# First four output blocks of four projections computed side by side over the input tiles, and the opening's conditioning rows in two channel halves

## The reference, cut to what matters

```python
for l in range(2):
    cond = silu(c) @ w_ada[l] + b_ada[l]              # 1024 -> 3 x 1024
    shift, scale, gate_raw = split(cond, 3)
    h = x * (1 + scale) + shift
    proj = h @ w_in[l]                                # 1024 -> 6272 columns
    p_hg, p_rw, p_gate = split(proj)                  # p_rw: r, k, v, z, decay/icl rank
    ...                                               # HGRN2, RWKV7 scans, branches
    x = layer_norm(DN_ALPHA * x + (1 + gate_raw) * (merged @ w_out[l]))
h = rms_norm(x); u = h @ lru_w_in                     # 1024 -> 2 x 1536
xb = conv4(u[:1536]); ...                             # RG-LRU, back to x
h = rms_norm(x); u = h @ ret_w_in; q, k = rotary(...) # retention, 4 heads, back to x
```

## Time and profile before

| | us |
|---|---|
| median of 3 runs | 2222.09 (2217.86 to 2224.73) |
| the profiled execution's own time | 2224.56 |
| its span | 2222.8 |
| PE busy | 1934.4 |
| DVE / ACT / POOL busy | 962.9 / 869.0 / 607.8 |

### The profile page before, as it was taken

The page is one execution under the profiler, slowest core; times in us unless marked ns, Lnnn a source line. Parts: engine busy times, 40 slices in busy tenths (PEclk is TensorE's granted clock), DMA queues, the critical chain, the costliest instruction groups (busy, mean ns, idle before and its releaser), DMA issues.

```text
span 2222.8 us, 35507 instructions
## 1 busy us (share of the span) xinstructions
PE 1934.4 (87%) x14368; PEld 1534.2 (69%) x14368; DVE 962.9 (43%) x1299; ACT 869.0 (39%) x1244; POOL 607.8 (27%) x255
## 2 busy tenths in 40 slices
PE   1999988899787998988899797989597998998987
PEld 1876877798565866877798574865474886777755
DVE  5326375632456126375632434737604123232232
ACT  1333456433323334456433324256515323333322
POOL 0333422200252433422300231422141441322212
PEclk9999999999898999999999899999799999999999
DMA  8232222200364322222200323211132231212112
GB/s 333 84 101 64 93 86 71 67 4 13 127 261 156 104 68 67 90 85 71 67 4 13 133 95 133 95 57 48 61 101 95 95 99 43 86 47 66 56 58 77
DMA packets 57524, 192.80 MB, mean 87 GB/s; under 512 B 5408, under 2 KB 5664, under 8 KB 54976
## 3 DMA queue, kind: packets, MB, share of 16 engines
q1 hardware_dynamic: 57408, 191.10, 25.5%
HBM read 173.25 MB, written 17.83 MB: 86 GB/s over the span
## 4 chain that ended last, share of the span: by engine, by line
issue 51%; PE 29%; POOL 9%; DVE 5%; ACT 3%; DMA 1%; POOLq 0%; DVEq 0%; ACTq 0%; SPq 0%
PE proj L1690 17%; POOL w_lo_sb L625 9%; PE aux L1850 2%; PE aux L1781 2%; DVE area_sb L1106 2%; DMA slots_sb<-w_ada 1%; PE aux L1907 1%; PE proj L1850 1%; PE aux L1904 1%; DVE area_sb L1109 1%; DVE slots_sb L1109 1%; ACT L720 1%; DVE act_lo_sb L1106 0%; DVE slots_sb L1106 0%; ACT L810 0%
## 5 line engine op out<-in xcount | busy, mean ns | idle before, releaser
L625 POOL TENSOR_TENSOR w_lo_sb<-w_raw_sb,w_hi_sb 128x1024 fp32r<-128x1024 f32 x231 | 589.6, 2553 | 1404.1 <-ACT w_hi_sb L700 1404.1
L1690 PE MATMUL proj<-act_hi_sb,w_hi_sb 128*128 128x512 f32 x1784 | 730.3, 409 | 97.4 <-DVE act_lo_sb L1106 63.5
L1690 PE MATMUL proj<-act_lo_sb,w_hi_sb 128*128 128x512 f32 x1784 | 707.3, 396 | 0.0
L1690 PE MATMUL proj<-act_hi_sb,w_lo_sb 128*128 128x512 f32 x1784 | 707.2, 396 | 0.0
L700 ACT ACTIVATE w_hi_sb<-w_raw_sb 128x1024 fp32r<-128x1024 f32 x231 | 244.4, 1058 | 740.4 <-PE proj L1690 687.0
L1690 PEld LDWEIGHTS proj<-act_hi_sb,w_hi_sb 128*128 128x128 f32 x1784 | 343.1, 192 | 192.3 <-issue 63.0
L1690 PEld LDWEIGHTS proj<-act_lo_sb,w_hi_sb 128*128 128x128 f32 x1784 | 343.3, 192 | 74.0 <-issue 6.3
L1690 PEld LDWEIGHTS proj<-act_hi_sb,w_lo_sb 128*128 128x128 f32 x1784 | 342.5, 192 | 74.2
L1106 DVE TENSOR_TENSOR area_sb<-area_sb 128x256 f32<-128x256 f32 (+2 forms) x208 | 141.3, 718 | 20.0 <-ACT area_sb L835 11.8
L1106 DVE TENSOR_TENSOR slots_sb<-slots_sb 128x512 f32<-128x512 f32 (+1 forms) x64 | 73.7, 1155 | 64.1 <-ACT slots_sb L795 26.1
L1106 DVE TENSOR_TENSOR area_sb<-area_sb,slots_sb 128x512 f32<-128x512 f32 (+1 forms) x90 | 72.1, 816 | 49.7 <-ACT slots_sb L722 38.7
(11 more groups left out here) (234 smaller groups left out, 2328.1 us busy)
## 6 DMA issues: line engine op xcount, KB each, us to landing
w_raw_sb<-wall SPq DMA_DIRECT2D x231, 512.0 KB, 3.5
slots_sb<-w_ada SPq DMA_DIRECT2D x8, 1536.0 KB, 7.3
slots_sb<-w_ada SPq DMA_DIRECT2D x8, 1024.0 KB, 5.9
gate_scr<-stage_sb SPq DMA_DIRECT2D x32, 256.0 KB, 2.2
slots_sb<-gate_scr SPq DMA_DIRECT2D x32, 256.0 KB, 4.0
x_scr<-area_sb SPq DMA_DIRECT2D x3, 2048.0 KB, 7.5
area_sb<-x_scr SPq DMA_DIRECT2D x3, 2048.0 KB, 9.5
area_sb<-x_t SPq DMA_DIRECT2D x2, 2048.0 KB, 9.6
```

The costliest lines, as they stand in the source:

```text
L625: nc.gpsimd.tensor_tensor(w_lo[:, b % 2, :, :].rearrange("p k n -> p (k n)"), w_raw[:, b % 2, :], w_hi[:, b % 2, :, :].rearrange("p k n -> ...
L1690: ins = MM(bank, w[:, s, k, :], a[:, t, :], start=(start and i == 0), stop=(stop and i == len(terms) - 1))
```

## The change

In four places (rw in layers 0 and 1, `lru_in`, the first head's `ret_in`) the first four output blocks are computed together. Their weights are laid out anew: piece p of the group holds input tiles 2p and 2p + 1 of all four blocks. TensorE takes input tile after input tile and does its three terms for all four blocks, 12 matmuls, into four `aux` banks (`project_group`); it counts a piece as used behind every second tile. The block of `w_down` and `a_down`, first until now, becomes the fifth. ScalarE's calls of `weights` for the group's third to fifth piece stand between its `high` calls, and the one for the sixth ahead of the four copies out. The loops lose one turn.

In the opening the shift and scale rows are loaded and added up in two halves of 512 channels each, eight parts of 512 KB a half, six buffers, x tile by tile between them. VectorE makes the first four tiles of h ahead of the second half's steps; TensorE's column sums of the second half stand between the group's fourth and fifth tile. The gate's columns come in two transfers, and its eight steps sit behind the first two blocks of each of three turns and two at the end. Elsewhere bank numbers and counts follow.

```diff
+    def side_by_side(blocks):
+
+        grouped.append(len(pieces))
+        return [[blocks[m][2 * p + k] for k in range(2) for m in range(4)] for p in range(4)]
...
-        rw = [full("w_in", l, 4096)]
+        rw = side_by_side([full("w_in", l, 2048 + P * m) for m in range(4)])
+        rw += [full("w_in", l, 4096)]
...
-        jobs.add(("ada", l), 0)
+        for half in range(1 if l else 2):
+            jobs.add(("ada", l, half), 4 + half)
+        for i in range(4):
+            jobs.add(("rw", l, i), i, signalled=False)
...
-            return b if b < first["lru_out", 0][0] else b - 4
+            return b - 4 * sum(b > g for g in grouped) - 4 * (b >= first["lru_out", 0][0])
...
+        def group_ready(eng, name):
+
+            eng.wait_ge(block_used, first[name[:2]][0] + 4)
+            return aux[jobs(name)[0]][:, :]
...
-            sp.dma_start(xa[:, :, :], dram["x_t"].rearrange("k p t -> p k t")).then_inc(S("x_in"), 16)
-
-            def load_ada(l, k):
-                n = 8 * l + k
-                wait(sp, S("ada_used"), n - 1)
-                cols = slice(0, ADA if l else 2 * D)
-                sp.dma_start(ada_in[:, k % 2, cols], dram["w_ada"][l, k][:, cols]).then_inc(S(f"ada_in{k % 2}"), 16)
-
+
+            def load_part(half, k):
+                n = KT * half + k
+                wait(sp, S("ada_used"), n - 5)
+                sp.dma_start(ada_part[:, n % 6], dram["w_ada"][0, k][:, D * half:D * half + D])\
+                    .then_inc(S(f"ada_part{n % 6}"), 16)
+
+            def load_x(m):
+                sp.dma_start(xa[:, m, :], dram["x_t"][m]).then_inc(S(f"x_first{m}"), 16)
+
+            def load_ada(k):
+                wait(sp, S("ada_used"), 2 * KT + k - 1)
+                sp.dma_start(ada_in[:, k % 2], dram["w_ada"][1, k]).then_inc(S(f"ada_in{k % 2}"), 16)
+
+            for k in range(6):
+                load_part(0, k)
+            load_x(0)
+            load_x(1)
+            blocks_to(1)
+            load_part(0, 6)
+            load_part(0, 7)
+            load_x(2)
+            load_x(3)
+            blocks_to(2)
             for k in range(KT):
-                if k == 6:
-                    blocks_to(2)
-                load_ada(0, k)
+                load_part(1, k)
+            for m in range(4, KT):
+                load_x(m)
...
-                    sp.dma_start(hg.rearrange("p (k h) t -> p k (h t)", k=KT),
-                                 dram["w_ada"][0].rearrange("k p n -> p k n")[:, :, 2 * D:]).then_inc(S("gate_cols"), 16)
+                    for half in range(2):
+                        sp.dma_start(hg[:, 8 * half:8 * half + 8].rearrange("p (k h) t -> p k (h t)", k=4),
+                                     dram["w_ada"][0, 4 * half:4 * half + 4].rearrange("k p n -> p k n")[:, :, 2 * D:])\
+                            .then_inc(S("gate_cols"), 16)
+                        blocks_to(6 + half)
...
@@ ScalarE
+                    if m > 2 and m % 2:
+                        weights(b_rw + m // 2 + 1)
+                weights(b_rw + 5)
...
+                for i in range(4):
+                    x = group_ready(act, ("rw", l, i))
+                    if i > 1:
+                        evacuated_job(act, ("rw", l, i - 2))
+                    A(ST[(b_rw + i) % 2], x, ACT.Copy, scale=V(f"mu{l}", 1 + i)).then_inc(S("mu_scaled"), 1)
+                for i in (2, 3):
+                    evacuated_job(act, ("rw", l, i))
+                b = b_rw + 4
...
+            for i in range(4):
+                x = group_ready(act, ("lru_in", 0, i))
+                act.wait_ge(S("conv_done"), i + 1)
+                job_read(A(ST[(LRU + i) % 2], x, ACT.Copy), ("lru_in", 0, i))
...
@@ VectorE
+            conditioned(0, 0, ((0, 4), (8, 4)))
+            for m in range(5):
+                if m < 4:
+                    modulated(0, m)
+                if m:
+                    low(SPLITS["h", 0] + m - 1, m - 1, ST[(m - 1) % 2])
+            for k in range(KT):
+                ada_part_step(1, k)
...
-                with dve.Fori(0, 4) as turn:
+                    dve.wait_ge(S("gate_cols"), 32)
+                with dve.Fori(0, 3) as turn:
                     for j in range(4):
-                        shifted(b + j, 1 + j, slots[:, turn, j, :], turn)
-                        if l == 0 and j % 2:
-                            k = 2 * turn + j // 2
+                        shifted(b + j, 5 + j, slots[:, turn + 1, j, :], turn)
+                        if l == 0 and j < 2:
+                            k = 2 * turn + j
                             dve.wait_ge(S("gate_rows"), k + 1)
                             stt(xa[:, 4:6, :], hg[:, bass.ds(2 * k, 2), :], derived[:, bass.ds(derived_column("c") + k, 1)], xa[:, 4:6, :],
                                 ALU.mult, ALU.add).then_inc(S("gate_rows"), 1)
+                if l == 0:
+                    for k in (6, 7):
+                        dve.wait_ge(S("gate_rows"), k + 1)
+                        stt(xa[:, 4:6, :], hg[:, 2 * k:2 * k + 2, :], DV["c"][:, k:k + 1], xa[:, 4:6, :],
+                            ALU.mult, ALU.add).then_inc(S("gate_rows"), 1)
...
+            for j in range(4):
+                evacuated_job(dve, ("lru_in", 0, j))
+                convolved(X_C[:, j, :], (LRU + j) % 2, [V("conv_w", RT * k + j) for k in range(4)], V("conv_b", j))
+            with dve.Fori(0, RT // 4 - 1) as turn:
...
@@ TensorE
+            def project_group(phase, layer, ready):
+
+                b = first[phase, layer][0]
+                banks = [job_open(pe, (phase, layer, i)) for i in range(4)]
+                for k in range(KT):
+                    s = (b + k // 2) % 2
+                    ready(k)
+                    if k % 2 == 0:
+                        pe.wait_ge(lo_ready, b + k // 2 + 1)
+                    pe.wait_ge(split_lo, SPLITS[("h", layer) if phase == "rw" else phase[0:3] + "_h"] + k + 1)
+                    for i in range(4):
+                        at = 4 * (k % 2) + i
+                        for n, (w, a) in enumerate(((w_hi, act_hi), (w_hi, act_lo), (w_lo, act_hi))):
+                            ins = MM(banks[i], w[:, s, at, :], a[:, k, :], start=(k == 0 and n == 0),
+                                     stop=(k == KT - 1 and n == 2))
+                    if k % 2:
+                        used(ins)
...
-                pe.wait_ge(S("ada_used"), 8 * (l + 1))
-                x = job_open(pe, ("ada", l))
-                for j in range(24 if l else 16):
-                    ins = MM(x[:, j:j + 1], ada_acc[:, P * j:P * j + P], C("ones", 0, 1), start=True, stop=True)
-                job_full(ins, ("ada", l))
-                used(project(b_rw, fresh=SPLITS["h", l]))
-                b = b_rw + 1
+                def condition(half):
+
+                    tiles = range(24) if l else range(8 * half, 8 * half + 8)
+                    pe.wait_ge(S("ada_used"), KT * (3 if l else half + 1))
+                    x = job_open(pe, ("ada", l, half))
+                    for j in tiles:
+
+                        at = j if j > 15 else 8 * (j % 8 // 4) + 4 * (j // 8) + j % 4
+                        ins = MM(x[:, at:at + 1], ada_acc[:, P * j:P * j + P], C("ones", 0, 1), start=True, stop=True)
+                    job_full(ins, ("ada", l, half))
+
+                condition(0)
+                project_group("rw", l, lambda k: condition(1) if (l, k) == (0, 4) else None)
+                used(project(b_rw + 4))
+                b = b_rw + 5
...
+            project_group("lru_in", 0, lambda k: None)
...
+    ada_cols = [D * s + HALF * half + np.arange(HALF) for half in range(2) for s in range(2)]
+    w_ada = a["w_ada"][:, :, np.concatenate(ada_cols + [np.arange(2 * D, ADA)])].reshape(DEPTH, KT, P, ADA)
...
```

More of the change, by code:

```diff
@@ L59, in block_plan @@
         add("out", l, [full("w_out", l, P * m) for m in range(8)])
-    add("lru_in", 0, [full("lru_in", 0, P * m) for m in range(2 * RT)])
+    add("lru_in", 0, side_by_side([full("lru_in", 0, P * m) for m in range(4)])
+        + [full("lru_in", 0, P * m) for m in range(4, 2 * RT)])
     tiles = [t for m in range(8) for t in full("lru_out", 0, P * m, RNN)]
@@ L149, in loop @@
         for name, bank in names:
[L150 removed]
+            self.table[name] = (bank, at[bank], per[bank], at[bank] - self.unsignalled[bank])
             at[bank] += 1
@@ L971, in _ @@
                 high(SPLITS["lru_h"] + m, m, ST[m % 2])
-            with act.Fori(0, RT // 4) as turn:
-                for j in range(4):
+                if m > 2 and m % 2:
+                    weights(LRU + m // 2 + 1)
+            weights(LRU + 5)
+            for i in range(4):
+                x = group_ready(act, ("lru_in", 0, i))
+                act.wait_ge(S("conv_done"), i + 1)
+                job_read(A(ST[(LRU + i) % 2], x, ACT.Copy), ("lru_in", 0, i))
+            with act.Fori(0, RT // 4 - 1) as turn:
+                for j in range(4, 8):
                     b = LRU + j
@@ L1042, in _ @@
```

(7 more changed lines are left out.)

195 lines of the change are left out of this document (113 added, 82 removed).

## The result

The changed kernel takes 2225.0 us (median of 20 runs, 2218.85 to 2231.75), the kernel before, beside it, 2221.02 us (20 runs, 2211.27 to 2225.73): ratio 1.0022, 95% interval 1.0011 to 1.0032. The forecast was 2224.3 us.

The account below looks back on a forecast made before the run. TensorE's matmuls, busy 87% of the span, were taken to bound the kernel. The terms -16.4 + 1.2 + 8.3 + 5.4 + 3.7 = +2.2 us gave 2226.8 profiled, 2224.3 against the runs' median; range 2209 to 2234.

Parts of the forecast that it names:

- Opening, -16.4: Opening: the first four blocks end at 61.8 us instead of 78.2, a gain of 16.4 us, bounds 14.0 to 19.4.
- T0: Start of a group's matmuls; in the opening predicted at 27.1 us instead of 53.2.
- T1: Opening: when TensorE can go on with the group's second half, predicted at 48.5 us after 6 us idle.
- Gate rows, +1.2: Gate steps in the opening: one more step behind the last block lengthens a TensorE wait by 1.2 us, bounds 0 to 2.4.
- Rival C: Eight cold starts: the low clock lasts 1.5 us longer at each, +6 us, giving 2230.3 us; chance 0.20.
- Layer 1, +8.3: Layer 1: fifth block's load late behind SP's stop, 6.8 us idle, 2.0 for the clock, 0.7 gained by rearranging: +8.3 us.
- merely shared port: VectorE and GpSimd sharing bandwidth instead of one blocking the other: layer 1's stall about 5 us instead of 6.8.
- LRU, +5.4: LRU block: convolutions and copies delay later blocks, 5.3 us idle, 2.0 for the clock, less 1.9: +5.4 us.
- Retention, +3.7: Retention: fifth block's load behind the stop and the tables, 4.1 us idle, 1.5 for the clock, less 1.9: +3.7 us.
- Sum, +2.2: Whole kernel: the five places together add 2.2 us to the profiled execution's 2224.56 us.
- Rival B: Layer 1 and retention: loads land as lone ones do, idle 2.7 and 1.8 us, -7.7 in all, 2214.4 us; chance 0.20.
- B': Layer 1, LRU and retention: no stall at all, -19.5 us in all, 2202.6 us; chance 0.05.

Follow-up runs that it names:

- Experiment 2: The changed kernel with the fifth block's load moved ahead of SyncE's wait for the last low half, in layer 1 and retention: 2212.76 us, ratio 0.9969 to the kernel before.

## Why the prediction was right, step by step

The class was as forecast, and in four of the five places the mechanisms were the named ones. That the time came within a us of the median is partly luck: the change cost +4.9 us where I had +2.2, and the kernel before came out 1.1 us lower than the median that I had added to. The sizes, each as predicted and as the trace has it:

- *Opening, -16.4: -15.9.* T0 27.88 for 27.1, since VectorE's step on 1024 columns takes 1.28 us where I had halved 2.35. T1 49.91 for 48.5: the order (rounding, `high(4)`, GpSimd, `low(4)` held) came as written, but the load was late, and the rounding started at 45.73 where I had the landing at 44.2. The group ended at 62.25 for 61.8: behind T1 only six matmuls start 0.43 us or more apart, where I had twelve, and that won back most of the late start.
- *Gate rows, +1.2: +3.8. This step failed.* "One more step, 1.2 us" was right for the wait (idle 5.97 against 4.65), but I took the wait's own growth for the whole price. The other 2.5 us lie behind it, and I had put them at nothing: 0.5 in the small matmuls, where the granted clock over 11 us fell from 0.69 to 0.58; 0.8 given back at a weight wait; and 2.8 from a second wait for VectorE, 4.58 us for 3.33, and the matmuls behind it. Rival C has the low clock, with eight places, and these are not among them. Taking the first wait away brought 9.3 us in the trace, 5.5 of them below the kernel before (72.5 to 67.0), so most of its price was there before the change.
- *Layer 1, +8.3: +8.6.* SyncE's stop, `up` at T0 + 18.25 for 18.5, idle 7.21 for 6.8, nine slow matmuls behind it. Experiment 2 removes it by the order alone. The fifth block landed 8.0 us after its issue, not after the 3.5 of lone loads: at 721.0, 1.2 us behind the 1 MB of `v_scr` issued ahead of it. With that the trace agrees with the ring order of the Trainium skill, "DMA: Bandwidth & Descriptors", section "Queues, rings and completion order". The rows below bear on the port pair of the Trainium skill, "SBUF — State Buffer", section "SBUF: two separate sides", and agree: `low(4)`, 0.69 us by itself, starts 0.48 us into GpSimd's subtraction and ends 0.55 us past its end. That a merely shared port would have made the stall 5 us, as I wrote, stands on no row.

```profile
702.34 2.41 POOL L672 TENSOR_TENSOR w_lo_sb<-w_raw_sb,w_hi_sb 128x1024 fp32r<-128x1024 f32 x1 [31.41 <-ACT w_hi_sb L748]
...
702.82 2.48 DVE L1178 TENSOR_TENSOR act_lo_sb<-stage_sb,act_hi_sb 128x512 fp32r<-128x512 f32 x1 [5.67 <-ACT act_hi_sb L756]
```

- *LRU, +5.4: +3.6.* The chain is the one that I wrote down: third copy, fourth copy, rounding, third convolution held by GpSimd, the copy out. Three sizes were off. The convolution without GpSimd takes 2.8 us a block and not 3.3, so idle is 3.78 and not 5.3. The group's 96 matmuls take 23.2 us and not 24.2, 3.0 less than before where I had 1.9. Against that, the slow matmuls behind the stall cost 3.0 us and not 2.0.

```profile
1393.87 0.60 ACT L1036 ACTIVATE stage_sb<-aux 128x512 f32<-128x512 f32 x1 [4.25 <-DVE slots_sb L1181]
1396.69 0.60 ACT L1036 ACTIVATE stage_sb<-aux 128x512 f32<-128x512 f32 x1 [2.22 <-DVE slots_sb L1181]
1397.19 1.05 ACT L748 ACTIVATE w_hi_sb<-w_raw_sb 128x1024 fp32r<-128x1024 f32 x1
1401.41 0.60 ACT L1044 ACTIVATE stage_sb<-proj 128x512 f32<-128x512 f32 x1 [3.17 <-DVE slots_sb L1181]
...
1394.27 2.33 DVE L1181 SCALAR_TENSOR_TENSOR slots_sb<-stage_sb,vec_sb,slots_sb 128x512 f32<-128x512 f32 x3
...
1397.09 4.29 DVE L1181 SCALAR_TENSOR_TENSOR slots_sb<-stage_sb,vec_sb,slots_sb 128x512 f32<-128x512 f32 x3
```

- *Retention, +3.7: +3.1.* Idle 3.68 for 4.1, the clock behind it 1.7 for 1.5, the group 2.2 us shorter for 1.9.
- *Sum, +2.2: +3.2 in the trace, +4.9 (2.4 to 7.1) by the runs.* The errors of the gate (2.6 low) and the LRU block (1.8 high) nearly cancel; the sum is better than its terms.

Rival B (no stall of full size) and B' (none) fell with the row at 724.64. Rival C, the longer low clock, is not seen at the cold starts that I counted: behind the three stalls nine, thirteen and nine matmuls take about 0.43 us each, where I had allowed twelve. Low clock at places that I had not counted is seen at the column sums, and in the scatter.

Two things that I took for granted went wrong in the expectations, not in the forecast: that a group whose loads come in time is worth nothing in retention (4 us in its stretch), and that its worth would be alike in both places.

## What to carry to other kernels

An instruction that looks free in its queue, such as a load behind a wait that is always long past, is only free in this order of work: when the work ahead of it is rearranged, look at what stands behind every such wait. Rearranging for the tiles and moving the load gave +8.6 us and +0.8 us in the same place. And price a wait of TensorE with the stretch behind it, up to the next place that is the same in both kernels: here the wait's own growth was 1.3 of 3.8 us.

## What I had not expected of the hardware

- A stretch with a wait of 5.97 us ahead of small matmuls is 9.3 us longer than the same without it: 6.1 us up to the wait's end, 1.2 in the 32 matmuls behind it, 0.4 further on, and 1.6 behind another wait, of 4.58 us in both. The granted clock over the 11 us behind the first wait was 0.58, and 0.84 with it gone.
- Eight matmuls of 32 rows take 3.69 us at a granted clock of 1.00, or 7.19 at 0.50, in profiles of the same program part; a stretch with no edit moves by 5 us. One profiled pair can therefore show -5.7 us where twenty runs each show +4.
- A VectorE operation on four columns took 1.77 us, ten times its own time, ending with GpSimd's subtraction.
